# A two-layer and one-layer network in one kernel: the first attention takes six weight products between its steps, its search starts as soon as its indexer is ready, and the modulation halves load over two queues

## What is computed

```python
mod = (cond @ ada_w[l] + ada_b[l])          # 1024 x 6144 per layer
sh_m, sc_m, g_m, sh_f, sc_f, g_f = jnp.split(mod, 6, axis=-1)
h = x * (1.0 + sc_m) + sh_m
q, k, v, qi, ki, wi, bg, cg, xb = _split(h @ w_in, EVEN_SIZES)
# attention, per block of 128 rows, 8 heads of 64:
rel = relu(einsum('bthd,bsd->bths', qi, ki)); score = einsum('bths,bth->bts', rel, wi)
_, idx = lax.top_k(where(admissible, score, NEG), 64)
p = softmax(q @ k[idx] * scale - slopes * dist)       # only the 64 keys found
ya = p @ v[idx]
yb = bg * causal_dwconv(cg * xb, conv_w)     # 3 taps, width 512
x = layer_norm(ALPHA * x + (1.0 + g_m) * (concat([ya, yb]) @ w_out), ...)
```

## Time and profile before

| | us |
|---|---|
| median of 3 runs (1249.76 to 1258.08) | 1252.72 |
| the profiled execution | 1247.78 |
| its span | 1245.7 |
| PE busy over the span | 1155.2 |
| DVE, ACT, POOL busy over the span | 559.4, 582.8, 827.4 |

### The profile page before, as it was taken

One profiled execution on the slowest core, in us unless ns is written; L12 is line 12 of the kernel. 1 busy time (PEld: TensorE's weight loads), 2 busy tenths in 40 slices (PEclk: granted clock), 3 DMA queues, 4 the chain that ended last, 5 costly groups with the idle time before them and its releaser, 6 DMA issues.

```text
span 1245.7 us, 21662 instructions
## 1 busy us (share of the span) xinstructions
PE 1155.2 (93%) x8119; PEld 1043.1 (84%) x8119; DVE 559.4 (45%) x1149; ACT 582.8 (47%) x868; POOL 827.4 (66%) x290
## 2 busy tenths in 40 slices
PE   6899798999999876999999989999999998999996
PEld 2799687999996873989999959999998987999995
DVE  4359666766557886375322372224211234111113
ACT  0443525554542435354554515455777543554452
POOL 3567448988882730689888825656565765988884
PEclk9899989999998988999999998999999998999998
DMA  9788567999984350678655523444444553666661
GB/s 342 262 292 231 187 209 233 345 335 320 301 301 151 98 136 1 220 227 263 202 179 175 170 65 93 144 135 137 136 139 136 187 165 103 194 192 183 188 185 67
DMA packets 253193, 237.69 MB, mean 191 GB/s; under 512 B 18043, under 2 KB 216496, under 8 KB 253136
## 3 DMA queue, kind: packets, MB, share of 16 engines
q1 hardware_dynamic: 237312, 202.80, 52.6%
q10 hardware_dynamic: 14784, 31.98, 7.1%
q0 software_dynamic: 1040, 2.12, 0.5%
HBM read 235.83 MB, written 1.05 MB: 190 GB/s over the span
## 4 chain that ended last, share of the span: by engine, by line
PE 72%; DVE 8%; ACT 7%; POOL 5%; DMA 5%; issue 2%; SPq 0%; DVEq 0%; POOLq 0%; ACTq 0%
PE bank L1147 18%; PE bank L1148 18%; PE bank L1149 18%; POOL unit_lo L688 5%; ACT unit_hi L790 3%; DMA raw<-in_ev_w_in 2%; PE bank L1186 2%; PE bank L1172 2%; PE bank L1174 2%; PE bank L1218 2%; PE bank L1206 1%; DMA att<-in_ada_w 1%; PE bank L1208 1%; PE bank L1226 1%; PE bank L1327 1%
## 5 line engine op out<-in xcount | busy, mean ns | idle before, releaser
L688 POOL TENSOR_TENSOR unit_lo<-raw,unit_hi 128x2048 fp32r<-128x2048 f32 (+4 forms) x88 | 349.3, 3973 | 261.0 <-ACT unit_hi L790 260.9
L1147 PE MATMUL bank<-h_hi,unit_hi 128*128 128x256 f32 x1248 | 354.2, 284 | 0.3
L1148 PE MATMUL bank<-h_lo,unit_hi 128*128 128x256 f32 x1248 | 353.5, 283 | 0.0
L1149 PE MATMUL bank<-h_hi,unit_lo 128*128 128x256 f32 x1248 | 353.4, 283 | 0.0
L722 POOL TENSOR_TENSOR unit_lo<-raw,unit_hi 128x2048 fp32r<-128x2048 f32 (+1 forms) x70 | 257.2, 3675 | 70.5 <-ACT unit_hi L922 66.9
L1147 PEld LDWEIGHTS bank<-h_hi,unit_hi 128*128 128x128 f32 x1248 | 239.6, 192 | 5.0 <-issue 1.3
L1148 PEld LDWEIGHTS bank<-h_lo,unit_hi 128*128 128x128 f32 x1248 | 239.6, 192 | 2.7
L1149 PEld LDWEIGHTS bank<-h_hi,unit_lo 128*128 128x128 f32 x1248 | 239.6, 192 | 0.0
L790 ACT ACTIVATE unit_hi<-raw 128x2048 fp32r<-128x2048 f32 (+4 forms) x98 | 163.2, 1666 | 105.9 <-PE bank L1149 38.0
L725 POOL TENSOR_TENSOR down<-raw_down,down 128x1024 fp32r<-128x1024 f32 x70 | 176.2, 2517 | 0.0
L1862 DVE SCALAR_TENSOR_TENSOR work<-bank,cols,work 128x254 f32<-128x254 f32 (+1 forms) x176 | 72.7, 474 | 146.9 <-ACT work L909 146.9
(11 more groups left out here) (310 smaller groups left out, 2065.1 us busy)
## 6 DMA issues: line engine op xcount, KB each, us to landing
raw<-in_ffn_w_up SPq DMA_DIRECT2D x88, 512.0 KB, 5.2
raw<-in_w_in SPq DMA_DIRECT2D x60, 512.0 KB, 4.6
raw_down<-in_ffn_w_down SPq DMA_DIRECT2D x44, 512.0 KB, 4.9
raw<-in_w_up SPq DMA_DIRECT2D x64, 256.0 KB, 3.1
raw_down<-in_w_down SPq DMA_DIRECT2D x32, 512.0 KB, 3.5
raw<-in_ev_w_in SPq DMA_DIRECT2D x28, 512.0 KB, 5.3
ada<-in_ada_w ACTq DMA_DIRECT2D x13, 1024.0 KB, 7.8
att<-in_ada_w SPq DMA_DIRECT2D x12, 1024.0 KB, 7.7
```

The lines of the kernel that those rows point to most:

```text
L688: nc.gpsimd.tensor_tensor(ul[g % 2][:, w], raw[g % 2][:, w], uh[g % 2][:, w].bitcast(F32), ALU.subtract).then_inc(lo_up, 1)
L1147: nc.tensor.matmul(o, sh, mh, start=first, stop=False)
L1148: nc.tensor.matmul(o, sh, ml, start=False, stop=False)
L1149: return nc.tensor.matmul(o, sl, mh, start=False, stop=last)
```

## The change

There are five parts.

- **PE**: QKV0 moves in front of the indexer products; the four pairs of indexer products come in two groups of two pairs with QKV1 between; QKV2 to QKV5 follow. CX0 to CX3 no longer stand before the attention; with BG0 and BG1 they are its fillers, in the halves (3, 1, 2, 1, 2, 1, 1, 1).
- **DVE**: halves 6 and 7 are summed before the indexer's sums, half 8 after the fourth head; the search follows the eighth with nothing between. The four convolutions and the four halves 9 to 12 lie inside the attention's steps. `out_low` stands in front of `normalize` of the same step. The output projection carries three halves in place of four, each behind the residual and not in front of it.
- **Banks**: all four outputs of the first attention take bank 6 (before, banks 6 and 7 in turn), since bank 7 holds running sums during the attention.
- **ACT**: waits for the positive parts stand behind other units' work; it takes up CX0 to CX3 inside the attention; it issues the transfers of halves 11 to 15 (`load_sum`) and of the gate rows. Each `load_sum(a)` waits in ACT's list until half a-2 is summed.
- **SP and POOL**: SP issues halves 6 to 10, each behind a unit, and the larger part of the constants, which POOL issued before.

```diff
-                turn(("pv", a, h // 2), 6 + h // 2 % 2)
+                turn(("pv", a, h // 2), 6 if a == DSA else 6 + h // 2 % 2)
...
-        FILL = {DSA: [[(G_BG[0], 0), (G_BG[0], 1)], [(G_BG[1], 0)], [(G_BG[1], 1)], [], [], [], [], []],
+        FILL = {DSA: halves(G_CX + G_BG, (3, 1, 2, 1, 2, 1, 1, 1)),
...
         DONE = {a: [[g for g, part in fill if part == 1] for fill in f] for a, f in FILL.items()}
-        DONE[DSA] = [[], [], [G_BG[0]], [], [G_BG[1]], [], [], []]
...
-        SUM_IDX = {0: [6], 2: [7], 4: [8], 6: [9]}
-        SUM_CONV = [10, 11]
-        SUM_EVEN = [12, 13, 14, 15]
+        SUM_EARLY = [6, 7]
+        SUM_IDX = 8
+        SUM_ATT = [9, 10, 11, 12]
+        SUM_EVEN = [13, 14, 15]
...
-            for g in range(2, G_QKV[DSA][2]):
+            early = {G_KI: SUM_EARLY[0], G_QKV[DSA][0]: SUM_EARLY[1], G_QKV[DSA][2]: SUM_IDX, G_QKV[DSA][3]: SUM_ATT[0],
+                     G_QKV[DSA][4]: SUM_ATT[1]}
+            for g in range(G_KI, G_EO[-1] + 1):
                 load_unit(g)
-            for h in range(HEADS):
-                if h % 2 == 0:
-                    load_unit(G_QKV[DSA][2 + h // 2])
-                for a in SUM_IDX.get(h, []):
-                    load_ada(a)
-            for i, g in enumerate(G_CX + G_BG):
-                load_unit(g)
-                if i < 2:
-                    load_ada(SUM_CONV[i])
...
+                if g in early:
+                    load_ada(early[g])
+                if g == G_QKV[DSA][1]:
+                    i1 = CONST_AT["ones"][1]
+                    sp_.dma_start(cst[:, i1:], consts[:, i1:]).then_inc(const_in, 16)
...
+                    if p and a == DSA:
+                        out_high(a, p - 1)
                     for g in DONE[a][2 * p + 1]:
                         filler(g)
-                    if p:
+                    if p and a != DSA:
                         out_high(a, p - 1)
...
+            evac_qkv(G_QKV[DSA][0], 0, 0)
...
-                if h % 2 == 0:
-                    evac_qkv(G_QKV[DSA][h // 2], 0, h // 2)
-            for j in range(4, 6):
+                if h == 3:
+                    evac_qkv(G_QKV[DSA][1], 0, 1)
+            for j in range(2, 6):
                 evac_qkv(G_QKV[DSA][j], 0, j)
...
-            attention(DSA, gated)
+            def load_sum(a):
+
+                act.wait_ge(ada_acc, a - 1)
+                act.dma_start(ada[a % 2].rearrange("p (t n) -> p t n", t=KD // 2), ada_half(a)).then_inc(ada_in[a % 2], 16)
+
+            AHEAD = {2: SUM_ATT[2], 3: SUM_ATT[3], 5: SUM_EVEN[0]}
+
+            def even_filler(g):
+
+                (cg if g < G_BG[0] else gated)(g)
+                if g == G_CX[1]:
+                    for w in range(2):
+                        load_gates(act, 0, w)
+                if g - G_CX[0] in AHEAD:
+                    load_sum(AHEAD[g - G_CX[0]])
+
+            attention(DSA, even_filler)
             load_rows(0, W["ln_mix_g"][0:1, :], W["ln_mix_b"][0:1, :])
-            for g in G_EO:
+            load_sum(SUM_EVEN[1])
+            for j, g in enumerate(G_EO):
                 other(g)
+                if j == 1:
+                    load_sum(SUM_EVEN[2])
...
+            unit_cols(G_QKV[DSA][0], hh, hl)
...
-                unit_cols(G_QKV[DSA][p], hh, hl)
+                if p == 1:
+                    unit_cols(G_QKV[DSA][1], hh, hl)
+            for g in G_QKV[DSA][2:4]:
+                unit_cols(g, hh, hl)
             for g in G_QKV[DSA][4:6]:
                 unit_rows(g, hh, hl)
-            for g in G_CX:
-                unit_cols(g, hh, hl)
...
+                    if p and a == DSA:
+                        out_low(a, p - 1)
                     for h in (2 * p + 2, 2 * p + 3) if p + 1 < PAIRS else ():
                         normalize(a, h)
+                    if middle:
+                        middle(p)
                     for h in (2 * p + 4, 2 * p + 5) if p + 2 < PAIRS else ():
                         soft(a, h)
-                    if p:
+                    if p and a != DSA:
                         out_low(a, p - 1)
...
-            for a in SUM_FIRST:
+            for a in SUM_FIRST + SUM_EARLY:
                 modulation_half(a, bank[7][:, :])
...
+                if h == 3:
+                    modulation_half(SUM_IDX, bank[7][:, :])
...
-            unit_evacuated(dve, G_CX[-1])
+
+            def gate(i):
+
+                g = G_BG[i]
+                o = unit_full(dve, g)[:, :].rearrange("p (k t) -> p k t", k=2)
+                for b in (2 * i, 2 * i + 1):
+                    unit_evacuated(dve, G_CX[b])
+                V.tensor_tensor(o, o, ybc[:, 2 * i:2 * i + 2, :], ALU.mult).then_inc(bg_ready, 1)
+                dve.wait_ge(yb_hi, i + 1)
+                V.tensor_tensor(yl[:, 4 + 2 * i:6 + 2 * i, :], o, yh[:, 4 + 2 * i:6 + 2 * i, :].bitcast(F32),
+                                ALU.subtract).then_inc(unit_free(g), 1)
+
+            def dsa_middle(p):
+
+                if p < 3:
+                    convolution((0, 2, 3)[p])
...
+
+                if p == 0:
+                    convolution(1)
+                if p >= 2:
+                    gate(p - 2)
+                modulation_half(SUM_ATT[p], bank[7][:, :])
+
+            attention(DSA, dsa_between, dsa_middle)
...
-            mixer_residual(G_EO, 0, lambda j: modulation_half(SUM_EVEN[j], bank[7][:, :]))
+            mixer_residual(G_EO, 0, lambda j: [modulation_half(a, bank[7][:, :]) for a in SUM_EVEN[j:j + 1]])
```

More of the change, by code:

```diff
@@ L738, in _ @@
             lo_unit(1)
[L739 to L742, removed]
             for g in range(2, G_EO[-1] + 2):
@@ L978, in _, with cg @@
                 nc.scalar.activation(b[:, 0:384], b[:, 0:384], ACT.Relu).then_inc(idx_relu, 1)
-                if h % 2 == 0:
-                    evac_qkv(G_QKV[DSA][h // 2], 0, h // 2)
-            for j in range(4, 6):
+                if h == 3:
+                    evac_qkv(G_QKV[DSA][1], 0, 1)
+            for j in range(2, 6):
                 evac_qkv(G_QKV[DSA][j], 0, j)
-            def cg(i, g):
-                b = unit_full(act, g)
+            def cg(g):
+                i, b = g - G_CX[0], unit_full(act, g)
                 if i >= 2:
@@ L989, in cg @@
                 hi_unit(g + 2)
-            for i, g in enumerate(G_CX):
-                cg(i, g)
             def gated(g):
@@ L1804, in out_low, with attention @@
                                 ).then_inc(free(("pv", a, p)), 1)
-            def attention(a, between=None):
+            def attention(a, between=None, middle=None):
                 for h in range(4):
@@ L1821, in attention, with mixer_residual @@
                 out_low(a, PAIRS - 1)
-            def mixer_residual(gs, w, before=None):
+            def mixer_residual(gs, w, between=None):
                 for j, g in enumerate(gs):
-                    if before:
-                        before(j)
                     o = unit_full(dve, g)[:, :].rearrange("p (t n) -> p t n", t=TT)
@@ L1837, in mixer_residual @@
                         ins = chunk_statistics(tt, j, UC)
+                    if between:
+                        between(j)
                 link(ins)
@@ L1988, in _ @@
                 ins.then_inc(free(("idx", h)), 1)
-                for a in SUM_IDX.get(h, []):
-                    modulation_half(a, bank[7][:, :])
+                if h == 3:
+                    modulation_half(SUM_IDX, bank[7][:, :])
             evacuated(dve, ("idx", HEADS - 1))
@@ L2002, in _, with convolution @@
                 link(V.tensor_tensor(m, m, C("dist_chunk")[:, P:S] if tt == 0 else C("dist_chunk"), ALU.add))
-            for b, g in enumerate(G_CX):
+            def convolution(b):
+                g = G_CX[b]
                 o = unit_full(dve, g)
@@ L2016, in _ @@
                 ins.then_inc(unit_free(g), 1)
-                if b < 2:
-                    modulation_half(SUM_CONV[b], bank[7][:, :])
-            unit_evacuated(dve, G_CX[-1])
-            def dsa_between(p):
[L2022 to L2030, removed]
+            def gate(i):
[10 more added lines that the diff above has]
+                    convolution((0, 2, 3)[p])
+            def dsa_between(p):
+                if p == 0:
[4 more added lines that the diff above has]
+            attention(DSA, dsa_between, dsa_middle)
             mod_rows(0, 0)
             dve.wait_ge(x_in, 16)
-            mixer_residual(G_EO, 0, lambda j: modulation_half(SUM_EVEN[j], bank[7][:, :]))
+            mixer_residual(G_EO, 0, lambda j: [modulation_half(a, bank[7][:, :]) for a in SUM_EVEN[j:j + 1]])
             mod_columns(0, (1,), (0, 0))
```

5 lines of the change are left out of this document (removed).

## The result

Four runs of the changed kernel took 1232.6 to 1243.3 us, median 1237.9, beside 1253.9 for the kernel before (four runs as well): a ratio of 0.9876 (95% interval 0.9848 to 0.9905), 12 to 19 us faster. The forecast was 1239.1. The profiled execution took 1237.4 us, its span 1235.4.

What follows compares the result with a forecast made beforehand. PE was taken to bound the first attention's stretch: EO0 17.6 us earlier at the floor, less new waits, leaves 13.6 us gained after the projection. 1252.7 - 13.6 = 1239.1 us on the median's scale; 8-in-10 range 1232 to 1250.

Steps and rivals of the forecast that it cites:

- the floor up to the scores: From KI's end at 59.85 us, PE work of 39.2 us puts the first attention's first scores at 99.0.
- The transfers rival: Transfers run late first between KI and CX0 (18 us), second in the output projection (8): 12 slower, 1265; chance 0.07.
- "nothing": Rival: the stretch is bound by something unseen (POOL, HBM), so moved products only wait elsewhere: 1252 us; chance 0.07.
- the list of new waits: PE waits in the filled attention and EO0: 0.9, 0.2, 1.7 and 1.4 us on top of the floor.
- 0.9 ahead of `weighted(1)`: PE's second multiplication by the values waits 0.9 us for `out_low`, since all outputs share bank 6.
- 0.2 ahead of `weighted(2)`: ACT's `load_sum` of half 12 needs half 10 summed, delaying copies and output 1; PE waits 0.2 us.
- 1.7 ahead of `weighted(3)`: After BG1, PE waits 1.7 us for `out_low`, behind DVE's division, convolution, gate and half 11.
- 1.4 in EO0: EO0 gets through 14 products, then waits 1.4 us for the last quarter, from the last `out_low`.
- one of my signs of being wrong: A granted clock of 0.5 anywhere from 100 to 175 us was to show the forecast wrong.
- The clock rival: PE's waits of 1.7 and 1.4 us drop the clock, losing 3.6 us twice: gain 6, 1246 us; chance 0.05.
- The search: DVE's search takes 17.8 us, ends at 98.2 before the scores, and stays hidden with 4 us to spare.
- The long-chain rival: DVE's closed chain through ACT in the attention costs 4 to 8 us more: gain 7, 1246 us; chance 0.15.

Runs made afterwards that it cites:

- experiment 2: Changed kernel with CX0 to CX3 multiplied ahead of the attention again, only BG0 and BG1 left as fillers (also called conv_ahead); 1249.9 us, ratio 0.9968.
- experiment 10: Changed kernel with halves 11 to 15 on SP's queue, convolution(3) before the last divisions, and gate-row broadcasts behind BG0 instead of CX1; 1230.5 us, ratio 0.9824.
- 4: Changed kernel with convolution(3) moved ahead of normalize(6) and (7) on DVE; 1237.3 us.
- 9: Changed kernel with halves 11 to 15 on SP's queue and convolution(3) ahead of normalize(6) and (7); 1235.6 us.
- experiment 1: Changed kernel run again unaltered, for a second profile; 1238.1 us, ratio 0.987.
- experiment 7: Changed kernel with halves 11 to 15 on SP's queue, computing only the last of four additions in halves 9 to 12; one run, 1236.9 us.
- 11: Changed kernel, halves 11 to 15 still issued by ACT, with convolution(3) before the last divisions and gate-row broadcasts behind BG0; 1236.3 us, ratio 0.9882.
- 5: Changed kernel with ACT issuing the two ln-row broadcasts behind EO1 instead of behind the attention; median 1238.5 us.
- 3: Changed kernel with halves 11 to 15 issued by SP's queue instead of ACT's; 1234.9 us, ratio 0.9856.
- experiment 6: Changed kernel with halves 11 to 15 on SP's queue, convolution(3) earlier, halves 8 to 15 summed in SBUF, outputs alternating between two banks; 1251.0 us.

## Why the prediction came out

**The mechanism held.** Taking back the fillers loses 12 of the 16 us (experiment 2, with the bank still shared). The queues, the new order of `out_high` and `out_low` and the constants were not tested by themselves against the kernel before. PE met the floor up to the scores: 98.7 for a forecast of 99.0. EO0 came at 150.6 for 147.8, EO3 at 177.4 for 174.3. The transfers rival fell between KI and CX0 (no PE wait there at 252 GB/s, where I had it decide from 290 downward), and "nothing" fell.

**The gain in the profile was over-sized by 3 us:** 10.6 measured for 13.6. Two terms were mis-sized: the list of new waits (5.7 us in all for 4.2), and the clock, which the sum had at nothing. I had waits of 0.9, 0.2, 1.7 and 1.4 us.
- 0.9 ahead of `weighted(1)`: 2.1. I had costed the gate rows on ACT's queue at nothing. They hold up BG0's weights, and moving them removes the wait (experiment 10).
- 0.2 ahead of `weighted(2)`: none.
- 1.7 ahead of `weighted(3)`: 0. In its place PE waits 2.5 us ahead of BG1 for bank 4, which `convolution(3)` frees. I had followed the outputs' bank and not the units'; experiments 4 and 9 show it: with that convolution earlier, the waits are 0.8 and none. The forecast wait was only hidden behind this one: in 9 and 10 it appears, with 1.5 and 1.8 us.
- 1.4 in EO0: 1.1.
- The clock fell to 0.67 from 140 to 145 us, and in it to 0.50, the lower level, from 142 to 145, some 1.7 us lost. That was one of my signs of being wrong. The clock rival thus happened in small in this execution; with the same 2.5 us wait in experiment 1 it did not (1.00). In 10 a wait of 1.8 us was followed by a clock of 0.62, in 9 waits of 2.1 and 1.5 us by 1.00. What decides it is not shown.

**The search** took 21.3 us for a forecast 17.8. The 2.37 us of its first addition in the earlier trace rows was already a hold by POOL (its split from 92.11 ended at 96.74), 2.1 us of it; without it the search is 15.7. After, three instructions are held, for 0.8, 1.4 and 3.4 us: 15.7 + 5.6 = 21.3. The 4 us to spare covered it.

**The long-chain rival** did not come about, and experiment 7 says why: DVE's sums set none of PE's waits up to EO0, only the 1.1 us inside it.

**The transfers rival** was right about its second place and wrong about its price. In the projection weights do come late in some executions, for 4 us and not 8. I had summed bytes over a mean rate. Nor do my prices follow from the 8 MB: these would be 10.6 us late at 225 GB/s and 2.6 at 290, not 8 and 5. What the runs show is that it takes both, half 13 and the ln rows. With half 13 issued 0.1 to 1.7 us ahead of EO2's weights and the rows within 1.2 us of them, ACT had these weights 13.4 to 14.1 us after their issue (experiments 1, 4 and 11). With only half 13 (5) or only the ln rows (3, 9 and 10, half 13 gone 4.6 to 4.9 us before) it was at most 9.0. The first profile, on the lucky side, had both behind the weights and does not show it. That transfers from any queue share the same engines, as the Trainium skill has it ("DMA: Bandwidth & Descriptors", section "Issuing engines are not separate DMA queues"), agrees with 10 and 11: over the projection 313 GB/s came with one queue and 283 with two. The second queue brought no bandwidth, only another order, and it cost 5.8 us.

**The median was met partly by offsetting errors.** I had put the profile of before 4.9 us under its median and assumed the same offset after. It was not there: the profiled pair differs by 10.4 us, the medians by 16 and 17. Over all runs, the mean granted clock of the kernel before was 0.961 (56 runs) and that of the changed one 0.967 (10 runs); the profiled pair had 0.965 and 0.964. Within the kernel before, a run gains about 0.54 us per 0.001 of clock (a fitted line). The difference of 0.006 would then be 3 us of these 6. That is a correlation; why the clock is higher, and the rest, stays open. Against the clock as the whole of it: conv_ahead (experiment 2) is 4 us under the kernel before at the same mean clock of 0.960, with a stretch that ended no earlier. Both profiles of the kernel before were among its fastest executions (1247.8 and 1245.1), so they may not show what its median runs lose.

## What to carry to other kernels

An attention whose chain leaves PE idle is best filled with independent products, but then follow every bank and every transfer that the moved engine work releases, not only the one you changed. A transfer whose issue hangs on one engine's progress overtakes another's as soon as that engine is faster: keep the urgent loads and the bulky ones in one list, in the order in which they are needed, and look at the next load behind one that you move out of the way (experiment 5). And take a second profile before trusting a quiet one.

## What the runs showed of the hardware

A DVE instruction that reads two operands from SBUF, or one comparison from SBUF to SBUF, does not slow down beside POOL's split but stands still until it ends: 0.29 us becomes 3.64, and a half's four additions that met two splits took 11.6 us instead of 3.1 (experiment 6). Additions with the running sum in a bank keep to 0.78 us beside such splits (from 118.42 in the profile after, three in 2.33 us, with a split until 119.55), and the search's `max` and `match_replace`, which read one operand from SBUF, keep to 0.43 and 0.41. The size does not matter to the standstill: an instruction of 128x8 that takes 0.16 us stood for 3.65, until the split of experiment 5 ended at 182.68. The Trainium skill ("SBUF — State Buffer", section "SBUF: two separate sides") calls it an exclusive lock on a shared pair of ports, held for the whole instruction; the trace agrees, with DVE's 101.05 behind POOL's 100.90 above. The first addition in the earlier trace rows was such a row, and I had read it as the price of the search.
